# Reciprocals written 64 times over for plain transposes in prompt attention, and three pooling tiles mixed inside the last down product

## The reference

```python
def _rms(x, g):
    y = x * lax.rsqrt(jnp.mean(x * x, axis=-1, keepdims=True) + 1e-6)
    return y * g

def _softmax_stats(s, sink):
    m = jnp.max(s, axis=-1)                       # with the sink of a head of group A
    p = jnp.exp(s - m[..., None])
    den = jnp.sum(p, axis=-1)
    return p, m, den                              # o = (p @ v) / den

def _pool_mixer(h_ctx, h, w_pool, pool_scale):    # layer 1
    ...
    # four channel groups: trailing mean over 2/4/8/16 tokens minus the token itself
    z = jnp.einsum('ntgc,gce->ntge', y, w_pool).reshape(n, t, D_MODEL)
    return z * pool_scale

def _sq_relu_mlp(x, w1, w2):
    return jnp.square(jax.nn.relu(x @ w1)) @ w2

# per layer:
xp = xp + _rms(mp, gl[1])                         # mp: attention or pooling mixer
xp = xp + _rms(_sq_relu_mlp(_rms(xp, gl[2]), w1, w2), gl[3])
```

## Times and profile before

| | us |
|---|---|
| median of 3 runs | 2305.12 (2304.23 to 2306.57) |
| the profiled execution's own time | 2304.14 |
| its span, first to last instruction | 2302.3 |
| PE busy | 2236.2 (97%) |
| DVE busy | 950.5 (41%) |
| ACT busy | 669.1 (29%) |
| POOL busy | 136.9 (6%) |

### The profile page before, as it was taken

The page is one execution under the profiler, slowest core; times in us unless marked ns, Lnnn a source line. Parts: engine busy times, 40 slices in busy tenths (PEclk is TensorE's granted clock), DMA queues, the critical chain, the costliest instruction groups (busy, mean ns, idle before and its releaser), DMA issues.

```text
span 2302.3 us, 34288 instructions
## 1 busy us (share of the span) xinstructions
PE 2236.2 (97%) x14129; PEld 2011.3 (87%) x14129; DVE 950.5 (41%) x1671; ACT 669.1 (29%) x1311; POOL 136.9 (6%) x202
## 2 busy tenths in 40 slices
PE   6999999998999999999999999989999999999998
PEld 6999877777789899898998997889989899898996
DVE  4210265566544334243342336573424334243346
ACT  4211486545333113021130223342203112031121
POOL 1000121000120000000000003230000000000001
PEclk9999999999999999999999999999999999999999
DMA  5221400099422112021020222221202112021123
GB/s 166 77 77 40 156 2 1 12 384 352 133 84 74 43 31 66 7 73 50 23 73 0 73 82 91 85 102 49 64 10 73 32 41 64 9 73 36 36 85 121
DMA packets 125778, 175.68 MB, mean 76 GB/s; under 512 B 14509, under 2 KB 94437, under 8 KB 125548
## 3 DMA queue, kind: packets, MB, share of 16 engines
q1 hardware_dynamic: 121500, 169.53, 22.4%
q10 hardware_dynamic: 4176, 4.72, 0.6%
HBM read 155.88 MB, written 18.58 MB: 76 GB/s over the span
## 4 chain that ended last, share of the span: by engine, by line
PE 75%; DVE 2%; DMA 1%; issue 1%; ACT 0%; SPq 0%; POOL 0%; DVEq 0%; POOLq 0%; ACTq 0%
PE ps L1701 32%; PE ps L1681 32%; PE ps L2535 4%; PE ps L2488 1%; DMA sa_va<-cache_a_v 1%; PE ps L1360 1%; PE ps L1690 1%; PE ps L1417 1%; PE ps L2505 1%; PE ps L1380 0%; DVE t_xn L1474 0%; DVE m_xT_lo L2304 0%; DVE t_zn L1474 0%; PE ps L2555 0%; SPq L655 0%
## 5 line engine op out<-in xcount | busy, mean ns | idle before, releaser
L1645 DVE TENSOR_TENSOR t_y<-t_y,ps 128x512 f32<-128x512 f32 x288 | 197.7, 687 | 627.3 <-PE ps L1701 627.2
L1701 PE MATMUL ps<-t_w_hi,t_h_hi 128*128 128x512 f32 x1152 | 450.3, 391 | 5.0 <-DVE t_y L1645 2.8
L1701 PE MATMUL ps<-t_w_lo,t_h_hi 128*128 128x512 f32 x1152 | 448.9, 390 | 0.0
L1701 PE MATMUL ps<-t_w_hi,t_h_lo 128*128 128x512 f32 x1024 | 399.1, 390 | 0.0
L1681 PE MATMUL ps<-m_xT_lo,t_w_hi 128*128 128x384 f32 x1488 | 328.0, 328 | 0.0
L1681 PE MATMUL ps<-m_xT_hi,t_w_lo 128*128 128x384 f32 x1488 | 328.0, 328 | 0.0
L1681 PE MATMUL ps<-m_xT_hi,t_w_hi 128*128 128x384 f32 x1488 | 327.9, 328 | 0.0
L1576 ACT ACTIVATE t_relu<-ps 128x384 f32<-128x384 f32 (+1 forms) x192 | 87.9, 458 | 809.8 <-PE ps L1701 776.7
L1606 DVE TENSOR_TENSOR t_w_lo<-t_raw,t_w_hi 128x1024 fp32r<-128x1024 f32 x128 | 155.4, 1224 | 276.7 <-ACT t_w_hi L1564 276.4
L1701 PEld LDWEIGHTS ps<-t_w_hi,t_h_hi 128*128 128x128 f32 x1152 | 216.7, 188 | 53.1 <-DVE t_y L1645 4.1
L1681 PEld LDWEIGHTS ps<-m_xT_hi,t_w_hi 128*128 128x128 f32 x1488 | 254.8, 188 | 1.1
(11 more groups left out here) (214 smaller groups left out, 2572.5 us busy)
## 6 DMA issues: line engine op xcount, KB each, us to landing
t_raw<-mlp_w SPq DMA_DIRECT2D x128, 512.0 KB, 4.0
sa_kb<-cache_b_k SPq DMA_DIRECT2D x40, 512.0 KB, 8.5
sa_vb_even<-cache_b_v SPq DMA_DIRECT2D x20, 512.0 KB, 12.1
sa_vb_odd<-cache_b_v SPq DMA_DIRECT2D x20, 512.0 KB, 11.2
in_raw<-attn_w_in SPq DMA_DIRECT2D x6, 1024.0 KB, 6.0
t_rows<-scratch_x SPq DMA_DIRECT2D x12, 512.0 KB, 5.7
qT<-x_prompt SPq DMA_DIRECT2D x8, 512.0 KB, 3.7
t_rows<-x_prompt SPq DMA_DIRECT2D x8, 512.0 KB, 3.5
```

Source lines behind the costliest of these rows:

```text
L1645: self.nc.vector.tensor_tensor(part, part, self.core.ps[:, 6 + n % 2, :], ALU.add).then_inc(self.part_added, 1)
L1701: mm = self.nc.tensor.matmul(self.core.ps[:, 6 + half, :], a[:, k, t * P:t * P + P], w[:, k, half * 512:(half + 1) * 512], start=(k == 0 a ...
```

## The change

In prompt attention the reciprocal becomes one instruction of 128x512: for each of the 8 heads the same denominator is read 64 times, through a broadcast input, and 64 equal reciprocals are written to a new tile `pa_rden`. PE's 8 matmuls become 4 plain transposes of 128x128 of that tile. Since `pa_rden` exists once, DVE waits for the transposes of the spread before.

In the trunk `scale_weights` moves from POOL to DVE, behind the parts 1 and 2 of the last down product. The tiles 0 to 2 are mixed inside that product, after p = 5, 6 and 7, in the banks 4 and 5, and DVE does their `add_z` after the parts 12, 14 and 16, with a gain loaded early and scratch tiles of their own. The later order of PE, ACT, DVE and POOL is rewritten for six remaining tiles. SP issues one more load, of `early_gain`, behind the load of `pool_scale`.

```diff
@@ prompt_attention
-    rden = den
+    rden = core.at("pa_rden", base + Attend.LEAST + 1024, [P, NH * HD])
...
                 dve.wait_ge(exped, step)
-                nc.vector.reciprocal(rden[:, i, d:d + NH], den[:, i, d:d + NH]).then_inc(rden_ready, 1)
+                if step > NH:
+                    dve.wait_ge(turned, spread_index[step // NH - 2] + 1)
+                nc.vector.reciprocal(rden[:].rearrange("p (h d) -> p h d", h=NH),
+                                     den[:, i, d:d + NH].rearrange("p (h o) -> p h o", o=1).to_broadcast([P, NH, HD])
+                                     ).then_inc(rden_ready, 1)
...
                 for p in range(4):
-                    for half in range(2):
-                        d = 2 * (j - 3 + p) + half
-                        last = nc.tensor.matmul(core.ps[half * HD:(half + 1) * HD, 4 + n % 2, p * P:(p + 1) * P],
-                                                rden[:, i, d:d + 1].to_broadcast([P, HD]), core.identity[:],
-                                                start=True, stop=True)
+                    last = nc.tensor.transpose(core.ps[:, 4 + n % 2, p * P:(p + 1) * P], rden[:, p * P:(p + 1) * P],
+                                               core.identity[:])
@@ trunk, SP
             sp.dma_start(scale_b[:], ins["pool_scale"].partition_broadcast(P)).then_inc(scale_in, 16)
+            sp.dma_start(early_gain[:], gains[5].partition_broadcast(P)).then_inc(early_gain_in, 16)
@@ trunk, POOL
-            pool.wait_ge(weights_in, 16)
-            pool.wait_ge(scale_in, 16)
-            scale_weights(0)
-            scale_weights(1)
@@ trunk, DVE, finish0
-                if n == 3:
+                if n in (1, 2):
+                    scale_weights(n - 1)
+                elif n == 3:
                     m0.take_sample(dve)
...
+                    if n // 2 in (6, 7, 8):
+                        add_z(n // 2 - 6)
@@ trunk, PE
             def during_down(p):
                 for q in {4: (0,), 5: (1, 2), 6: (3,), 7: (4,), 8: (5,)}.get(p, ()):
                     pooling(q)
+                if 5 <= p < 5 + EARLY_Z:
+                    mix(p - 5)
...
-            mix(0)
             pooling(6)
-            mix(1)
+            mix(3)
             pooling(7)
-            mix(2)
+            mix(4)
             pooling(8)
-            mix(3)
+            mix(5)
             pe.wait_ge(yT_ready, NT)
-            mix(4)
-            for q in range(5, NT):
-                turn(q - 5)
-                mix(q)
+            turn(0)
+            turn(1)
+            mix(6)
+            turn(2)
+            mix(7)
+            turn(3)
+            mix(8)
```

More of the change, by code:

```diff
@@ L758, in is_spread @@
         return groups[n][2] == 0
+    spread_index = [n for n in range(len(groups)) if is_spread(n)]
     def before(n):
@@ L1456, in __init__, with square @@
         self.scaled = core.sem(tag + "scaled")
-    def square(self, nc, act, x, q, rows=slice(0, P)):
+    def square(self, nc, act, x, q, rows=slice(0, P), junk=None):
         if q >= 1:
             act.wait_ge(self.squared, q)
-        nc.scalar.activation(self.junk[rows], x, ACT.Square, scale=1.0 / 32,
+        nc.scalar.activation((self.junk if junk is None else junk)[rows], x, ACT.Square, scale=1.0 / 32,
                              accum_out=self.ms[rows, q:q + 1]).then_inc(self.squared, 1)
@@ L1890, in turned_ps @@
     def turned_ps(q):
-        return core.feature_banks(6 if q in (5, 7) else 2)
+        return core.feature_banks(6 if q in (5, 7) else 0 if q in (1, 3) else 2)
+    EARLY_Z = 3
     def z_of(q):
-        return core.banks(4 + 2 * (q % 2), 2)
+        return core.banks(4 if q < EARLY_Z else 4 + 2 * (q % 2), 2)
     def columns(q):
@@ L2056, in _ @@
             nc.gpsimd.memset(y[:], 0.0).then_inc(m0.y_zero, 1)
-            post0.root(core, pool, 0)
-            pool.wait_ge(weights_in, 16)
-            pool.wait_ge(scale_in, 16)
-            scale_weights(0)
-            scale_weights(1)
-            for q in (1, 2):
+            for q in range(3):
                 post0.root(core, pool, q)
@@ L2070, in _ @@
             for q in range(5, NT):
+                if q >= 6:
+                    post_pool.root(core, pool, q - 6)
                 post0.root(core, pool, q)
@@ L2073, in _ @@
             pre_pool.root(core, pool, NT - 1)
-            for q in range(NT):
+            for q in range(EARLY_Z):
+                pre1.root(core, pool, q)
+            for q in range(EARLY_Z, NT):
                 post_pool.root(core, pool, q)
-                if q >= 1:
+                if q > EARLY_Z:
                     pre1.root(core, pool, q - 1)
@@ L2286, in add_z, with scale_weights @@
                 yt = y[r, PLACES[q], :]
-                if q >= 2:
+                normed = early_zn if q < EARLY_Z else zn[:, q % 2, :]
+                if q == 0:
+                    dve.wait_ge(early_gain_in, 16)
+                elif q < EARLY_Z:
+                    dve.wait_ge(x3_added, q)
+                elif q == EARLY_Z:
+                    dve.wait_ge(post_pool.gain_in, 16)
+                elif q >= EARLY_Z + 2:
                     dve.wait_ge(x3_added, q - 1)
-                post_pool.scale(nc, dve, z_of(q)[r, :], zn[r, q % 2, :], q, r)
+                gain = early_gain if q < EARLY_Z else post_pool.gain
+                dve.wait_ge(post_pool.rstd_ready, q + 1)
+                nc.vector.scalar_tensor_tensor(normed[r], z_of(q)[r, :], post_pool.rstd[r, q:q + 1], gain[r], ALU.mult,
+                                               ALU.mult).then_inc(post_pool.scaled, 1)
                 dve.wait_ge(post_pool.scaled, q + 1)
-                nc.vector.tensor_tensor(yt, yt, zn[r, q % 2, :], ALU.add).then_inc(x3_added, 1)
+                nc.vector.tensor_tensor(yt, yt, normed[r], ALU.add).then_inc(x3_added, 1)
+            def scale_weights(k):
+                dve.wait_ge(weights_in, 16)
+                dve.wait_ge(scale_in, 16)
+                nc.vector.tensor_tensor(pool_w[:, k::2, :], pool_w[:, k::2, :],
+                                        scale_b[:].rearrange("p (g c) -> p g c", g=4), ALU.mult).then_inc(weights_scaled, 1)
             def next_input(q):
@@ L2417, in _ @@
                 finish0(n)
-            for q in range(NT + 3):
-                if q < NT:
-                    add_z(q)
-                if 1 <= q <= NT:
-                    next_input(q - 1)
-                if q >= 3:
-                    take_lo(q - 3)
-                if q == 4:
-                    m1.split_lo(dve, 0, 0)
+            for q in range(EARLY_Z):
+                next_input(q)
+            add_z(3)
+            add_z(4)
+            next_input(3)
+            for q in range(5, NT - 1):
+                add_z(q)
+                for t in (0, 1) if q == 5 else (q - 4,):
+                    take_lo(t)
+                next_input(q - 1)
+                if q == 6:
+                    m1.split_lo(dve, 0, 0)
+            add_z(NT - 1)
+            next_input(NT - 2)
+            take_lo(4)
+            take_lo(5)
+            next_input(NT - 1)
+            for q in range(6, NT):
+                take_lo(q)
             m1.split_lo(dve, 0, 1)
```

55 lines of the change are left out of this document (31 added, 24 removed).

## The result

The changed kernel takes 2363.76 us (median of 4 runs, 2361.53 to 2369.39), the kernel before 2305.85 us beside it (2304.23 to 2306.79): a ratio of 1.0259, 95% interval 1.0247 to 1.0271. It is 57.9 us slower. The prediction said 2337 us, 2314 to 2368: the sign and the mechanism were right, the size 27 us too small.

A forecast was written before the change was run, and what follows sets the result against it. PE, 97% busy, leads, but DVE's reciprocal ends PE's waits in attention and DVE bounds the trunk's tail. Attention 38.4 - 7 + 6, trunk -5: 2304.1 + 37.4 - 5 = 2336.5, median 1.0 above: 2337 us, range 2314 to 2368.

The forecast's parts named there:

- What bounds the stage: Prompt attention: PE leads (184 of 200 us), yet DVE, 59% busy, ends PE's wait exactly where the reciprocal stands.
- The rival that the ring takes it up: Prompt attention: DVE's free 81 us absorb the reciprocal, only four wide places lose 2.7 us each; 2304 us, chance 0.06.
- The reciprocal's price: DVE in prompt attention: 512 elements take 2.9 us, 2.7 more than now, from a slope of 5.33 ns an element.
- the dear rival: Prompt attention: the reciprocal takes 4.3 us, at eight times the normal pace; +59, 2364 us, chance 0.12.
- The path: Prompt attention: 8 places add all 2.7 us to PE's path, 8 add 2.1 after 0.6 taken up; together 38.4 us.
- The spread on PE: Prompt attention: four transposes replace eight matmuls, saving 0.51 us sixteen times, 8.2 us, of which 7 counted.
- The clock: Prompt attention: new PE waits bring slow-clock episodes of 1.5 us; four of sixteen taken, 6 us (bounds none and 24).
- The trunk: Last down product and tail: removed hole and earlier mixes make it 5 us faster (bounds -8 and -1).
- Pooling 6: Trunk: PE waits 1.4 us for its pool input, since DVE needs 7.6 us and PE wants it after 6.3.
- the hole that the change removes: End of the last down product: PE's 2.1 us wait and 1.6 us slow stretch behind it go, gaining 3.8 us.

The follow-up runs named there:

- b1_extra: Kernel before, plus a second reciprocal of 128x512 that nobody reads, PE left as it was: 2376.95 against 2305.38 us, ratio 1.0310.
- b2_extra_half: Kernel before, plus a second reciprocal of 128x256 that nobody reads, PE left as it was: 2342.03 us, ratio 1.0156.
- a4_act: Kernel before with the change's attention part, but 8 reciprocals as before, repeated by ACT one unit later: 2303.92 us, ratio 0.9990.
- b3: Kernel before with the change's attention part, its 512-element reciprocal split into four 128x128 instructions, one after each of four units: 2330.41 us, ratio 1.0110.
- a1: Kernel before with only the attention part of the change: 2360.02 against 2304.84 us, ratio 1.0244.
- a3: Kernel before with the change's attention part, but 8 reciprocals as before, repeated by a plain copy on DVE: 2307.64 us, ratio 1.0011.

## Why the prediction was right, and where its size failed

**What bounds the stage: right.** It was read from the earlier trace rows and not from the sums of the earlier trace rows: DVE was 59% busy and its reciprocal still lay on PE's path at all 16 places. The rival that the ring takes it up (2304) counted 11 us of new waits, so PE's idle time would have been near 25 us; it was 56.6.

**The reciprocal's price: right in kind, a term too small.** I took 2.9 us and it is 3.35. The slope of 5.33 ns came from instructions of 2 and 8 elements, and they are too short to show it: 166 ns at 2 elements lies above the line that holds from 8 to 512 elements, which gives 160 there. One element costs 6.25 ns. The 1.05 ns that the prediction calls a plain copy's element is a mixture: the 154 ns at 2 elements are an addition, and the 690 at 512 a copy out of PSUM; against it the reciprocal's element is about six. The copy within SBUF took 427 ns at 512, so against that one it is more. 0.45 us in 16 places is 7 us of the 27 missed. The Trainium skill (VectorE: DVE Perf Modes, First, the fixed hardware budget) has a repeat count of 8; the prediction's estimate from it was 4.3 us. The measurement decides: it lies between the slope of the short rows and that count, nearer to the slope. The total of the dear rival, 2364, was met, but not by its reason (4.3 us); that is chance.

**The path: right.** By its rule, 8 x 3.15 + 8 x (3.15 - 0.6) = 45.6; PE's idle time grew by 42.7. `b1_extra` and `b2_extra_half` agree within 3 us. Some 5 us of the 42.7 stand in the rows as waits for ACT before the spread (8.3 where 3.3 stood), which the rule doesn't have, so the agreement is of the sum and not of every place.

**The spread on PE: right.** -7 was taken, -6.0 measured in the changed kernel and -7.8 in `a4_act`, where the clock was up.

**The clock: the step that failed.** "I take four, 6 us" became 18.1 us. The episode of the earlier trace rows was a fair measure of one (1.5 us), but I counted too few and too short ones: the clock below 0.95 in 16 stretches of 8 us instead of 5 is not four episodes. Over `b3`, `b2`, `a1` and `b1`, PE's other work grew by 11.3, 12.4, 18.0 and 21.2 us beside 15.9, 21.5, 42.7 and 46.1 us of waits, 0.4 to 0.7 us for each microsecond of wait; with only 4 us of new waits it was 5.5 us (`a3`) and nothing (`a4`). My bounds for the term, 0 to 24, held it; for the value in them I leaned on the wait of 2.50 us at 428 behind which nothing was slow. The same trace has four waits of over 1.5 us in this stage: behind two the clock fell (1.98 and 2.27 us), behind two it didn't (1.73 and 2.50). By these rows half of the sixteen would have been the guess, and not a quarter: 8 x 1.5 = 12 us.

**The trunk: right at each place, wrong in the sum.** DVE waited 4.73 us for the scale, PE did not, and the 84 matmuls ran through. The two instructions took 1.28 and 1.23 us. Pooling 6 waited 1.28 us (1.4 predicted). What I did not give that wait is its second price: 5.11 and 5.50 instead of 3.48 and 3.55, 3.6 us. (The up product's 1.5 us behind a wait of 2.85 is no loss against the kernel before, which had as much.) I had written these two prices down for the hole that the change removes (2.1 us of wait, 1.6 of slow clock) and not for the waits that it makes. With pooling 6 out of the way the same code gives 5.6 us, the -5 predicted.

Of the 27 us, then, 7 are the reciprocal's price, 12 the clock, 4 the trunk, 1 the spread, and the path took 3 back: 21 to 22. The other 5 lie outside the places of the change (5.6 + 1.9 in the profiled execution, which was 2.0 above its median); no run gives their cause. The attention part alone was 55.2 us slower, the change 57.9; the trunk part alone has no loss to explain the difference of 2.7, and it is about the width of the two intervals. It stays open.

## What to carry to other kernels

Before an instruction is widened, look up or measure what one element of it costs, not what the instruction costs: a reciprocal repeated 64 times is 64 reciprocals, and 8 reciprocals with a plain copy of the results did the same in less than a fifth of the time (0.20 + 0.43 us). Price new waits of TensorE at their length and, where they come to 15 us and more, at about half again for the clock behind them; with only 4 us of them the clock cost nothing in one kernel and 5.5 us in another. Look for work that can be put ahead of a wait; here an exchange of two calls removed 1.1 us of waiting and gave 5. An engine that is 59% busy has room for short pieces between what others wait for, and none for a long one.

## What the runs showed of the hardware

- VectorE's fp32 reciprocal costs 6.25 ns an element from 8 to 512 elements a partition (198, 948, 1753, 3348 ns at 8, 128, 256 and 512; all but the first with a broadcast input).
- A plain fp32 copy of 512 elements with a broadcast input took 427 ns from SBUF to SBUF, and one of 512 elements 690 from PSUM. The Trainium skill (VectorE: DVE Perf Modes, Mode 2×_2P) gives the reason: with one source and both ends in SBUF, both read ports serve one tensor and two elements pass a cycle; the two rows agree.
- TensorE's granted clock was at its lower level (0.50, 1.2 GHz) behind waits of only 1.28 and 1.29 us that followed full work, at the same place in two kernels; after a wait of 2.1 us in the last down product it fell in the kernel before (36 matmuls in 10.04 us) and did not in `a4_act` (8.48 us). Whether a wait costs the clock is not decided by its length alone: in prompt attention the wait of 1.73 us was followed by half clock in `a4_act` and not in the kernel before, and those of 1.98 and 2.27 us, at the same places, the other way round.
- 128 useless transposes, 16.9 us of TensorE's time, made the stage 3.2 us shorter, all of it in the part where they filled waits of 1.7 to 1.9 us whole.
